# A turn moved next to the following task's scores in the second network's attention

## The reference

```python
proj = x @ w_in[l]
(h_a, b_a, c_a, uv, q, kc, vc, ksl, vsl, kw, vw, gl) = jnp.split(proj, split_points, axis=-1)
y_a = short_conv(h_a, b_a, c_a, conv_w[l])
y_b = gmlp_spatial(uv, gmlp_ln_g[l], gmlp_ln_b[l], gmlp_w[l], gmlp_b[l])
y_c = nsa_attention(q, kc, vc, ksl, vsl, kw, vw, gl,
                    ck_pe[l], ck_w1[l], ck_b1[l], ck_w2[l],
                    cv_pe[l], cv_w1[l], cv_b1[l], cv_w2[l])
mix = jnp.concatenate([y_a, y_b, y_c], axis=-1) @ w_out[l]
x = layer_norm(ALPHA * x + mix, ln2_g[l], ln2_b[l])
```

## Time and profile before

| | before |
|---|---|
| median of 3 runs | 1976.64 us |
| profiled execution | 1976.44 us |
| its span | 1974.6 us |
| TensorE matmul busy | 1962.4 us, 99% of the span |
| VectorE busy | 1249.1 us, 63% |
| ScalarE busy | 911.7 us, 46% |
| granted TensorE clock, mean | 0.999 |

### The profile page before, as it was taken

How to read it: one execution, slowest core, us unless ns; L and a number is a source line. 1 busy time by engine, 2 the same in 40 slices (tenths; PEclk the granted TensorE clock), 3 DMA queues, 4 the chain that set the end, 5 groups by cost and what they waited for, 6 DMA issues and landing times.

```text
span 1974.6 us, 32204 instructions
## 1 busy us (share of the span) xinstructions
PE 1962.4 (99%) x14032; PEld 1792.9 (91%) x14032; DVE 1249.1 (63%) x1760; ACT 911.7 (46%) x1215; POOL 98.6 (5%) x84
## 2 busy tenths in 40 slices
PE   8999999999999999999999999999999999999998
PEld 7888999999888899999999989899999998989997
DVE  6566656665756666655565568665556556776555
ACT  4445444444444555444444435544444444555442
POOL 0000001000100000100010020010010002001000
PEclk9999999999999999999999999999999999999999
DMA  7544566675454455686666656369666664746663
GB/s 284 185 143 143 176 209 193 198 213 192 171 171 145 133 187 198 194 253 184 192 196 189 192 172 172 107 197 264 178 180 202 188 191 152 193 119 193 188 186 105
DMA packets 421446, 361.87 MB, mean 183 GB/s; under 512 B 29424, under 2 KB 361528, under 8 KB 421304
## 3 DMA queue, kind: packets, MB, share of 16 engines
q1 hardware_dynamic: 421160, 359.74, 59.6%
q10 hardware_dynamic: 144, 0.07, 0.0%
HBM read 358.72 MB, written 1.05 MB: 182 GB/s over the span
## 4 chain that ended last, share of the span: by engine, by line
PE 99%; DVE 0%; DMA 0%; ACT 0%; issue 0%; DVEq 0%
PE ps L218 23%; PE ps L220 23%; PE ps L219 23%; PE ps L225 8%; PE ps L227 8%; PE ps L226 8%; PE ps L1546 2%; PE ps L1722 1%; PE ps L1657 1%; PE ps L1698 1%; PE ps L1674 1%; PE ps L1711 0%; DMA cst<-in_const 0%; PE ps L1845 0%; PE ps L1762 0%; PE ps L1818 0%
## 5 line engine op out<-in xcount | busy, mean ns | idle before, releaser
L2119 DVE TENSOR_TENSOR hl<-raw,hl 128x1024 fp32r<-128x1024 f32 (+2 forms) x535 | 722.5, 1384 | 377.4 <-ACT hl L1873 377.0
L218 PE MATMUL ps<-xt,hl 128*128 128x256 f32 (+1 forms) x2672 | 754.8, 282 | 0.0
L219 PE MATMUL ps<-xt,hl 128*128 128x256 f32 (+1 forms) x2672 | 746.2, 279 | 0.0
L220 PE MATMUL ps<-xt,hl 128*128 128x256 f32 (+1 forms) x2672 | 745.7, 279 | 0.0
L1873 ACT ACTIVATE hl<-raw 128x2048 fp32r<-128x2048 f32 (+1 forms) x338 | 613.8, 1824 | 217.1 <-PE ps L227 158.1
L218 PEld LDWEIGHTS ps<-xt,hl 128*128 128x128 f32 (+1 forms) x2672 | 500.9, 187 | 7.0 <-issue 3.0
L219 PEld LDWEIGHTS ps<-xt,hl 128*128 128x128 f32 (+1 forms) x2672 | 501.0, 188 | 3.1
L220 PEld LDWEIGHTS ps<-xt,hl 128*128 128x128 f32 (+1 forms) x2672 | 500.8, 187 | 0.2
L225 PE MATMUL ps<-hl,o 128*128 128x512 f32 x656 | 261.5, 399 | 0.3
L227 PE MATMUL ps<-hl,o 128*128 128x512 f32 x656 | 259.0, 395 | 0.0
L226 PE MATMUL ps<-hl,o 128*128 128x512 f32 x656 | 258.8, 394 | 0.0
(11 more groups left out here) (211 smaller groups left out, 1555.4 us busy)
## 6 DMA issues: line engine op xcount, KB each, us to landing
raw<-in_w_in SPq DMA_DIRECT2D x83, 1024.0 KB, 5.0
raw<-in_w_ffn_in SPq DMA_DIRECT2D x88, 512.0 KB, 5.1
raw<-in_ffn_gate SPq DMA_DIRECT2D x88, 512.0 KB, 3.9
raw<-in_ffn_up SPq DMA_DIRECT2D x88, 512.0 KB, 5.2
raw<-in_ffn_down SPq DMA_DIRECT2D x44, 1024.0 KB, 5.1
raw<-in_w_ffn_out SPq DMA_DIRECT2D x22, 1024.0 KB, 5.2
raw<-in_w_out SPq DMA_DIRECT2D x24, 512.0 KB, 4.6
raw<-in_w_branch_a SPq DMA_DIRECT2D x8, 1024.0 KB, 5.3
```

The costliest lines, as they stand in the source:

```text
L218: e.matmul(out, l[0], r[0], start=start, stop=False)
L219: e.matmul(out, l[0], r[1], start=False, stop=False)
L220: return e.matmul(out, l[1], r[0], start=False, stop=stop)
L2119: e.tensor_tensor(lo[:, c], m["raw"][:, k % NRAW, 0:n][:, c], hi[:, c].bitcast(F), ALU.subtract).then_inc(s.low.up(("low", k), *([("low", ...
```

## The change

The cost that the turn yielded (0.88) is added to the scores', and the turn yields 0. So in the list nothing that `mix` could put in stands between Tn-1, which ends slot n, and scale n and Sn+1, which begin slot n+1. Since `main` now yields two steps in a slot in place of three, two steps of `side` follow a step that costs over 2 (the scores, 2.18), one follows any other. The computation, the operations and their shapes stay the same.

```diff
-                yield SCORES
+                yield SCORES + 0.88
...
                 yield 0
                 ets = turned(ers, 1)
-                yield 0.88
+                yield 0
                 yield from at.until("v")
...
                 yield cost
-                x = next(side, IDLE)
-                if x is not IDLE:
-                    yield x
+                for _ in range(2 if cost > 2 else 1):
+                    x = next(side, IDLE)
+                    if x is not IDLE:
+                        yield x
                 full()
```

## The result

The changed kernel takes 1980.99 us (median of 11 runs, 1980.78 to 1981.84), the kernel before 1976.64 us beside it: 1.0022 times as long, with a 95% interval of 1.0015 to 1.0030. The interval lies clear of 1, and on both sides of the 0.2% that the prediction took as the least that can be told. The prediction was 1981.4. The profiled execution took 1980.79 us. Lines of the changed kernel have numbers one higher than before (the scores 1675, the turn 1699, the values 1723, the compressed branch's turn 1837, the copies 1971, the mask's last operation 2498, the gated MLP's readers 2132, `low` 2120).

The account below looks back on a forecast made before the run. TensorE was taken as the bound, hardly waiting. Waits of 4.05 us less a gain of 1.7 made each layer 2.4 us longer, 4.8 for both: 1981.4 us, range 1977.6 to 1983.8.

Parts of the forecast that it names:

- S5's wait: Scores of task 5 wait for ScalarE's two copies out of the banks the preceding turn filled: 1.45 us a layer.
- t0's wait: Turn of the first compressed branch waits for its mask on VectorE, behind the first half of `low`: 1.7 us.
- S3's wait: Scores of task 3 wait for VectorE's readers of the gated MLP's banks: 0.8 us, between 0 and 1.2.
- Rival 2: Scores of task 3 find their banks free: +3.1 us, 1979.7 us; chance 0.20 with cases like it.
- T3's wait: Turn of task 3 waits for the bank that the first compressed branch's turn filled: 0.1 us, between 0 and 0.3.
- The gain: TensorE's saving from fewer borders between small and linear matmuls and no seeds wait: 1.7 us a layer, between 1.2 and 2.0.
- The adjacency: Four turns directly ahead of scores, which start 0.55 us behind the turn: 0.29 saved each, 1.2 us a layer.
- the seeds' part: First output part no longer waits for the seeds, listed a part earlier: about 0.2 us gained a layer.
- the other pairings: Fifth group of small matmuls saved and other steps newly paired or parted: 0.3 us gained, between 0 and 0.5.
- Rival 1: In the merged stage only the borders count and no wait forms: 1.7 us gained a layer, 1973.2 us; chance 0.08.
- bank waits alone: Only the waits for PSUM banks in the merged stage, 2.35 us a layer, none for the mask: +1.3, 1977.9 us.
- Rival 3: One more wait, the turn of task 5 for its scale: 0.5 to 1 us more a layer, 1982.4 to 1983.4; chance 0.14.

Follow-up runs that it names:

- early mask: Changed kernel with the first compressed branch's exponentials and mask listed with its maximum, ahead of the half of `low`: 1980.92 us, 1.0021 times the kernel before.
- The kernel without the three waits: Changed kernel with the sixth scores on dense banks, the gated MLP's turn yielding 1.0, not 0.5, and the first mask 1.4, not 0.9: 1974.06 us, 0.9986 times before.

## Why the prediction was right

The order that was worked out from the costs is the order in the trace, and the waits stand where they were put. By steps, in us a layer, start to start:

| step | predicted | changed kernel |
|---|---|---|
| S5 behind T3 | 2.00 | 1.98 (1257.02 to 1259.00) |
| t0, counted from S4 | 8.22 | 8.18 (1255.38 less 1247.20) |
| T3's own arrival | 9.84, free at 9.96 | 9.82, no wait |
| S3, counted from S0 | 21.2 | 21.20 (1238.91 less 1217.71) |
| waits together | 4.05 | 3.84 |
| gain | 1.7 | 1.44 (waits less 2.40) |
| sum | 2.4 | 2.40 |

**S5's wait**, 1.46 against 1.45 (1.98 less the 0.52 of a pair without a wait), was read off two rows of before: the turn's start and the end of its two copies. The experiment with the other banks took 1.43 and 1.46 away and changed nothing else, so the cause is shown, not only the size.

**t0's wait**, 1.66 against 1.7, follows from a chain that starts at S4 and could be copied from the rows of before, since no engine's order between S4 and the mask was changed. The early mask took it away.

**S3's wait**, 0.72 against 0.8, came from the longest walk, with two estimates in it. Its end point was good to 0.1: the last reader ends at 1238.76, 21.05 after S0, where 21.0 was put. From the half of `low` on, the steps are those of the walk, none off by more than 0.2. Its first leg was right by luck: VectorE is not idle between S0's maxima (1218.96) and the end of the maxima of task 1 (1227.18), so its own queue set the pace there and not the exponentials of task 0, and both came out alike. The list of what would show it gave T1 and S3 the 0.55 of a free pair, against the sum's own wait of 0.8; 1.24 is what the sum says. Rival 2 would have had S3 free; it falls. Eight linear parts lie between S0 and S3, before as after, and do not cover that walk.

**T3's wait** was given 0.1 and is 0: T3 starts 0.06 behind the end of its bank's reader (1256.28 + 0.68), where 0.16 was allowed for. In the early-mask kernel, where t0 is not late, it is 0.51.

**The gain** is the term that was mis-sized: 1.44, not 1.7. The adjacency itself was right or a little better (0.52 from turn to scores, not 0.55: 4 x 0.32 = 1.28), and the seeds' part came, since no wait is left ahead of the first output part (0.2 was put; in before that part starts 0.43 behind the last matmul of 256 columns, 0.31 more than a step). That leaves nothing for the other pairings, where 0.3 was put: 1.44 - 1.28 - 0.2 = -0.04, or somewhat less with 0.3 for the seeds. The timelines show two of them that cost. By the prediction's own way of counting a group, T2 c0, V1 and S4 cost 4.21, c0 V1 and T2 S4 cost 3.99: a gain of 0.22, not of 0.32, since c0 lost its place behind a turn. And `out`, from its start to the next step's, takes 0.63 ahead of T1, where behind S3 it took 0.46, and has a border of its own ahead. So "one border more or less" was the right width, and its middle was no gain, not one border. The kernel without the three waits says nearly the same: 1.34 and 1.31 a layer, with 0.23 of another wait in it. The busy time fell by 0.82, not by about 1.5: of the gain, 0.14 had been idle time before, and T lasts 0.71 and scores directly behind it start after 0.52, so where they wait the first 0.19 counts as busy. Of the 3.84 that the waits cost from start to start, 3.37 are idle time.

The two errors, 0.21 in the waits and 0.26 in the gain, cancel; that the sum is better than its terms is luck. **Rival 1** (only the borders count) falls for this kernel, and comes near where the waits are taken away: 1974.06 us there, in a somewhat other order, and 1973.2 in the prediction. What a border costs depends on what stands on its two sides. In before a turn of half arrays stands directly ahead of a product on the whole array:

```profile
1225.69 0.71 PE L1698 MATMUL ps<-cst,er 64*128 64x64 f32 x16
1226.33 1.10 PE L1818 MATMUL ps<-sg,v 128*128 128x64 f32 x8
```

These are 0.64 apart, as a turn and a linear matmul are the earlier trace rows; half-array scores come after 0.52. So to stand next to another small step is not enough by itself. The rule of the Trainium skill named with rival 1 ("TensorEngine Tiling (Array Packing)", section Tiling Modes), that a change of the tiling mode drains TensorE, agrees with these 0.64 and 0.52; the drain itself no row shows. **The other rule of the Trainium skill** (same title, section Performance Considerations, that tiling does not speed up the emptying of PSUM) bears on S5's wait, which is one for the copies of T3's banks, and which other banks took away. The prediction's time by bank waits alone was 1977.9; t0's wait, which is not for a bank, accounts for the rest. **Rival 3** falls: no wait stands ahead of T5 (1269.82, directly behind V4).

## What to carry to other kernels

When two steps of a full engine are pushed together, the parts that stood between them were the cover of something: list for each step that now comes earlier who fills, empties or masks what it needs, and count that chain from the last point that the change leaves alone, not from the step's old start. A step that directly follows a producer should not take the producer's own PSUM banks where others are free; which banks it gets is the allocator's choice and may be the cheapest thing to change. Raising one cost in a planner moves many steps, so a wait that is taken away by costs should be looked for at other places afterwards.

## What the runs showed of the hardware

The granted clock of TensorE fell to 0.51 and 0.63 in two stretches of 2 us, near its lower level, without any idle time longer than 1.24 us ahead of it in its stage: behind 0.51 and 1.24 us with 0.7 us of work between them (the 16 transposes of a turn), in one layer of two with the same waits, in both profiles of that kernel. The Trainium skill ("TensorE: Matmul & The Clock Gate", section What's actually happening) says that the gate goes by how busy TensorE was lately; the trace agrees as far as that the fall came behind waits and went when S5's wait was taken away. It nearly doubled the price: two waits of 1.75 us together cost a further 1.5. In the changed kernel longer waits (1.59 and 1.26) cost nothing beyond themselves.

A turn of half arrays and half-array scores directly behind it have no gap: 0.52 from start to start, 0.03 less than the earlier trace rows gave for the turn and the compressed scores, and 0.12 less than from a turn to a product on the whole array (0.64).
